# One layer of a hybrid Fourier, state-space and expert-retrieval model on one core: the context's tail reordered, the latents' first Fourier product moved behind the scores

## The reference

```
h     = RMSNorm(x) * (1 + scale1) + shift1
proj  = h @ w_in             # Fourier | z | x,B,C | dt | two gates
a_out = Re(DFT2(proj[Fourier])) @ w_fourier
y     = RMSNorm(SSD(x,B,C,dt) * silu(z)) ; b_out = y @ w_ssd_out
mix   = (sigmoid(gate_A) * a_out + sigmoid(gate_B) * b_out) @ w_out
x     = x + gate1 * RMSNorm(mix)
h     = RMSNorm(x) * (1 + scale2) + shift2
# retrieval, 8 heads: scores of two halves, top 16 of each, top 16 of their 256 sums
act   = gelu(<expert_u[idx], h>) ; out = sum(softmax(top) * act * expert_v[idx])
x     = x + gate2 * RMSNorm(out)
```

## Time and profile before

| | |
|---|---|
| median of 3 runs | 2580.18 us |
| the profiled execution | 2583.05 us, span 2581.2 us |
| granted clock of TensorE, mean | 0.956 |
| busy, share of the span | PE 89%, PEld 56%, DVE 70%, ACT 25%, POOL 46% |
| DMA | 705.28 MB, mean 273 GB/s |

### The profile page before, as it was taken

The page is one execution under the profiler, slowest core; times in us unless marked ns, Lnnn a source line. Parts: engine busy times, 40 slices in busy tenths (PEclk is TensorE's granted clock), DMA queues, the critical chain, the costliest instruction groups (busy, mean ns, idle before and its releaser), DMA issues.

```text
span 2581.2 us, 26507 instructions
## 1 busy us (share of the span) xinstructions
PE 2300.2 (89%) x8779; PEld 1451.1 (56%) x8779; DVE 1797.7 (70%) x3184; ACT 635.8 (25%) x1564; POOL 1179.9 (46%) x979
## 2 busy tenths in 40 slices
PE   6988888898899997999989999978799999999960
PEld 1545454454566443487668887856566666644420
DVE  2657676645600789778778898899676767657678
ACT  2325435231211113411322112199111111110010
POOL 0022231221000346667542235477557786876865
PEclk8999999999999998999999999999899999999985
DMA  8211101107585678999874578999999999999997
GB/s 308 74 33 58 41 24 41 49 33 296 164 284 178 213 298 324 370 369 413 320 268 160 223 280 322 351 365 412 417 379 419 378 411 409 383 400 372 414 389 288
DMA packets 235577, 705.28 MB, mean 273 GB/s; under 512 B 22910, under 2 KB 47614, under 8 KB 234052
## 3 DMA queue, kind: packets, MB, share of 16 engines
q0 software_dynamic: 117936, 429.44, 43.1%
q1 hardware_dynamic: 116948, 272.27, 28.4%
q10 hardware_dynamic: 576, 2.10, 0.2%
HBM read 690.23 MB, written 13.50 MB: 273 GB/s over the span
## 4 chain that ended last, share of the span: by engine, by line
PE 31%; DVE 22%; POOL 17%; DMA 15%; issue 11%; ACT 3%; SPq 1%; DVEq 0%; ACTq 0%; POOLq 0%
PE bank L960 13%; POOL arena L1785 7%; POOL arena L1777 7%; DMA arena<-in_peer_v,arena 6%; DMA arena<-in_peer_u,arena 6%; PE bank L809 4%; PE bank L854 2%; DVE arena L2205 2%; DVE arena L2183 2%; DVE arena L1966 2%; PE bank L1112 2%; POOL arena L1834 2%; DVE arena L2129 2%; DVE arena L2126 2%; DVE arena L2128 1%
## 5 line engine op out<-in xcount | busy, mean ns | idle before, releaser
L1777 POOL DMA_INDIRECT arena<-in_peer_u,arena x384 | 489.1, 1274 | 577.7 <-DVE arena L2183 326.5
L2205 DVE SCALAR_TENSOR_TENSOR arena<-arena 128x1024 f32<-128x1024 f32 x381 | 495.3, 1300 | 139.0 <-DMA arena<-in_peer_v,arena 134.3
L2183 DVE CUSTOM_DVE_ANT_0 arena<-arena 128x1024 f32<-128x1024 f32 x384 | 476.4, 1247 | 150.2 <-DMA arena<-in_peer_u,arena 149.6
L1785 POOL DMA_INDIRECT arena<-in_peer_v,arena x384 | 463.9, 1208 | 244.0 <-DVE arena L2205 136.8
L960 PE MATMUL bank<-arena 128*128 128x512 f32 (+1 forms) x1472 | 507.2, 507 | 15.3 <-DMA arena<-in_w_in 5.2
L1220 PE MATMUL bank<-arena 128*128 128x512 f32 x1024 | 452.3, 594 | 13.4 <-DVE arena L2381 9.3
L1182 PE MATMUL bank<-arena 128*128 128x256 f32 x2048 | 455.3, 380 | 7.1 <-ACT arena L1634 6.4
L1182 PEld LDWEIGHTS bank<-arena 128*128 128x128 f32 x2048 | 390.6, 191 | 88.4 <-issue 37.4
L960 PEld LDWEIGHTS bank<-arena 128*128 128x128 f32 x1472 | 282.4, 193 | 236.0 <-issue 201.1
L1220 PEld LDWEIGHTS bank<-arena 128*128 128x128 f32 x1024 | 195.0, 191 | 232.7 <-issue 214.4
L1634 ACT ACTIVATE arena<-bank 128x256 f32<-128x256 f32 x128 | 49.0, 383 | 589.4 <-PE bank L1182 589.4
(11 more groups left out here) (260 smaller groups left out, 2476.6 us busy)
## 6 DMA issues: line engine op xcount, KB each, us to landing
arena<-in_peer_ut SPq DMA_DIRECT2D x128, 512.0 KB, 6.5
arena<-in_peer_v SPq DMA_DIRECT2D x128, 512.0 KB, 6.6
arena<-in_w_in SPq DMA_DIRECT2D x22, 2048.0 KB, 8.1
arena<-in_w_ada_t POOLq DMA_DIRECT2D x32, 512.0 KB, 4.0
arena<-in_w_ssd_out SPq DMA_DIRECT2D x8, 2048.0 KB, 13.2
arena<-in_w_query SPq DMA_DIRECT2D x8, 2048.0 KB, 7.9
arena<-in_w_ada SPq DMA_DIRECT2D x4, 2048.0 KB, 16.3
arena<-in_w_fourier SPq DMA_DIRECT2D x4, 2048.0 KB, 7.7
```

What stands on the lines that cost most here:

```text
L1777: nc.gpsimd.indirect_dma_start(rowbuf[slot], None, a["peer_u"], bass.IndirectOffsetOnAxis(ap=entries(IDX, k), axis=0)).then_inc(row_in[slo ...
L1785: nc.gpsimd.indirect_dma_start(rowbuf[slot], None, a["peer_v"], bass.IndirectOffsetOnAxis(ap=entries(IDX, k), axis=0)).then_inc(row_in[slo ...
L2183: V.tensor_tensor_reduce(out=rowbuf[slot], in0=rowbuf[slot], in1=h2c if item < PH else h2a[:, item // PH - 1, :], scale=1.0, scalar=0.0, o ...
L2205: STT(pv, rowbuf[slot], w, pv, ALU.mult, ALU.add).then_inc(s("vc_used"), 1)
```

## The change

- The list of products: the latents' FO0 moves from behind the context's WO1 to behind its Q3. The products between change their numbers by one, and SP's loads follow.
- PE: after the Fourier stage there are no row vectors; the context's FO0 goes ahead of the transposes of Y, FO1 behind them. The four row vectors keep their order of use: kinds 0 and 1 ahead of the transposes of the merged rows, kinds 2 and 3 (four units) behind WO1, beside the norm. The latents' FO0 stands behind the scores.
- ACT: the copies move with them; kind 2 is copied between the first root and the square of x1, kind 3 behind the second root.
- DVE: the two dots of the last Fourier step come behind `put_fourier(7)`; the waits for the row vectors are split; 12 context steps stand beside the latents' FO0, three a tile, so the steps beside all later products shift by 12, and ACT's stops with them.
- Behind the scores of the latents 8 context steps are left beside the first two whole top-16 instead of 20 beside four, and the 32 apart steps stand at the third to the eighth (4, 4, 6, 6, 6, 6) instead of the fifth to the eighth (8 each).

```diff
-        + [("l", "FO0")] + [("c", f"Q{j}") for j in range(4)]
-        + [("l", n) for n in ("FO1", "GA0", ...) + STAGES]
+        + [("c", f"Q{j}") for j in range(4)]
+        + [("l", n) for n in ("FO0", "FO1", "GA0", ...) + STAGES]
-WITH = {"FO1": (2, 2, 2, 2), "GA0": (2, 2, 2, 2), ...
+WITH = {"FO0": (3, 3, 3, 3), "FO1": (2, 2, 2, 2), "GA0": (2, 2, 2, 2), ...
-CTX_BESIDE = (5, 5, 5, 5, 0, 0, 0, 0)
-APART_BESIDE = (0, 0, 0, 0, 8, 8, 8, 8)
+CTX_BESIDE = (4, 4, 0, 0, 0, 0, 0, 0)
+APART_BESIDE = (0, 0, 4, 4, 6, 6, 6, 6)
 ...
             pe.wait_ge(s("d2_free"), KT)
-            pe.wait_ge(s("coef_ready"), 3)
-            row_units(0, (2, 3), 0)
-            pe.wait_ge(s("row_free"), 4)
+            job("c", "FO0", f_lhs)
             for j in range(4):
                 pe.wait_ge(s("gt_used"), g_end("c", f"Z{j}"))
                 transpose_unit(T_YC + j, ...)
-            for j in range(2):
-                job("c", f"FO{j}", f_lhs)
+            job("c", "FO1", f_lhs)
 ...
             pe.wait_ge(s("coef_ready"), 5)
-            row_units(4, (0, 1), 0)
+            row_units(0, (0, 1), 0)
             pe.wait_ge(s("gt_used"), g_end("c", "SO3"))
-            pe.wait_ge(s("row_free"), 8)
+            pe.wait_ge(s("row_free"), 4)
 ...
             for j in range(2):
                 job("c", f"WO{j}", m_lhs)
-            job("l", "FO0", f_lhs)
+            row_units(4, (2, 3), 0)
             pe.wait_ge(s("h2_ready"), 1)
+            pe.wait_ge(s("row_free"), 8)
 ...
-            pe.wait_ge(s("tm_free"), q_end("l", "FO0"))
+            pe.wait_ge(s("tm_free"), q_end("c", "WO1"))
 ...
-            job("l", "FO1", f_lhs)
+            for j in range(2):
+                job("l", f"FO{j}", f_lhs)
 ...
@@ ACT
             root(slice(46, 47), ROOT_M[0])
+            take_rows(4, (2,), 0)
             square_x1(0)
             root(slice(51, 52), ROOT_N[0])
-            act.wait_ge(s("posm_in"), 16)
-            for i, t in enumerate(LAT4):
-                take(Q["l", "FO0"] + i, a_out(t, slice(0, 512)), ACT.Copy)
+            take_rows(6, (3,), 0)
 ...
+            act.wait_ge(s("posm_in"), 16)
+            for i, t in enumerate(LAT4):
+                between("l", "FO0", i)
+                take(Q["l", "FO0"] + i, a_out(t, slice(0, 512)), ACT.Copy)
@@ DVE
                 if f:
                     put_fourier(f - 1)
-                late_dots(DOTS_BESIDE_FOURIER[f])
+                if f < KT - 1:
+                    late_dots(DOTS_BESIDE_FOURIER[f])
             put_fourier(KT - 1)
-            late_dots(8)
+            late_dots(DOTS_BESIDE_FOURIER[KT - 1] + 8)
 ...
-            dve.wait_ge(s("row_free"), 8)
+            dve.wait_ge(s("row_free"), 4)
             add_mix(0)
+            dve.wait_ge(s("row_free"), 6)
             make_h2(0, mix_c, h2c)
             dve.wait_ge(s("sc_free"), 4)
             top(0)
             top(1)
-            for i in range(4):
-                beside("l", "FO1", i)
+            for j in range(2):
+                for i in range(4):
+                    beside("l", f"FO{j}", i)
```

More of the change, by code:

```diff
@@ L51 @@
 TAIL = ([("c", n) for n in ("Z0", "Z1", "Z2", "Z3", "FO0", "FO1", "GA0", "GA1") + STAGES]
-        + [("l", "FO0")] + [("c", f"Q{j}") for j in range(4)]
-        + [("l", n) for n in ("FO1", "GA0", "GA1", "Z0", "Z1", "Z2", "Z3") + STAGES]
+        + [("c", f"Q{j}") for j in range(4)]
+        + [("l", n) for n in ("FO0", "FO1", "GA0", "GA1", "Z0", "Z1", "Z2", "Z3") + STAGES]
         + [("l", f"Q{j}") for j in range(4)])
@@ L128 @@
 CSTEPS = PH * TOPK + LEAD
-WITH = {"FO1": (2, 2, 2, 2), "GA0": (2, 2, 2, 2), "GA1": (2, 2, 2, 2), "Z0": (2, 2, 2, 2), "Z1": (2, 2, 2, 2),
+WITH = {"FO0": (3, 3, 3, 3), "FO1": (2, 2, 2, 2), "GA0": (2, 2, 2, 2), "GA1": (2, 2, 2, 2), "Z0": (2, 2, 2, 2), "Z1": (2, 2, 2, 2),
         "Z2": (2, 2, 2, 2), "Z3": (2, 2, 2, 2), "GB0": (3, 3, 3, 3), "SO0": (2, 2, 2, 2), "SO1": (2, 2, 2, 2),
@@ L670, in _ @@
                 load_tail("c", name)
-            load_tail("l", "FO0")
             for j in range(4):
                 load_tail("c", f"Q{j}")
-            for name in ("FO1", "GA0", "GA1", "Z0", "Z1", "Z2", "Z3", "GB0", "SO0", "SO1", "GB1", "SO2", "SO3"):
+            for name in ("FO0", "FO1", "GA0", "GA1", "Z0", "Z1", "Z2", "Z3", "GB0", "SO0", "SO1", "GB1", "SO2", "SO3"):
                 load_tail("l", name)
@@ L1486, in _ @@
                 square_y(0, j)
[L1487 removed]
+            take(Q["c", "FO0"], a_out(0, slice(0, 512)), ACT.Copy)
             for j in range(4):
                 turned(T_YC + j, yTc[:, 4 * j:4 * j + 4, :], j)
[L1490 to L1491 removed]
+            take(Q["c", "FO1"], a_out(0, slice(512, 1024)), ACT.Copy)
             root(slice(30, 31), ROOT_Y["c"])
```

5 lines of the change are left out of this document (1 added, 4 removed).

## The result

| | before | after |
|---|---|---|
| median | 2579.56 us (4 runs) | 2595.82 us (4 runs, 2593.66 to 2599.43) |
| ratio | 1 | 1.0050, 95% interval 1.0026 to 1.0073 |
| profiled execution, span | 2583.05 us, 2581.2 us | 2594.78 us, 2593.0 us |

The changed kernel is slower by half a per cent: 12.9 us of 2580 by the ratio on record, 6.7 to 18.8 us by its interval; the two medians lie 16.3 us apart, inside it. The median of before counts one run more than the 2580.18 us ahead of the forecast. The forecast was 2583 us with a range of 2567 to 2597 us: the range holds the median, but the likeliest case (2576 to 2592 us) does not, and what came by the medians, "slower by over 0.5%" (a time above 2593.1 us), had 0.19.

What follows compares the result with a forecast made beforehand. The gather steps after the DVE-bound gate build set the end. PE 11.2 us late at the queries, less 6.4 at the squares, put the first gate multiply 3.8 us late: 2583 us median, range 2567 to 2597.

Steps and rivals of the forecast that it cites:

- the likeliest case: Whole kernel: DVE reaches item 2's gates late, PE stalls at Y's transposes; median 2583 us, 2576 to 2592 us, chance 0.52.
- slower by over 0.5%: Whole kernel: a time above 2593.1 us, from the slower case and the likeliest case's upper tail; chance 0.19.
- waits at the squares, PE's 6.38: Ahead of the build: ACT's 7.42 us wait for the squares goes, and with it PE's 6.38 us.
- PE's idle time: First transposes of Y: PE arrives near 984 us or a few later, idles some 20 us, resumes at 1006.9 us.
- The tail: Context's tail on PE: 4.8 us idle, 6.9 us row kinds and 1.0 us load wait saved; WO1 ends at 769.2 us.
- The norm: Behind WO1: h2's turn 9.9 us later, then 36.0 us plus 1.4 us for PE's clock; latents' FO0 at 816.5 us.
- DVE's way to item 2: From first top-16 to item 2's gates: 37.8 us of dots and adds plus 5.2 us more; reached at 999.2 us.
- the wait of step 20 stays: DVE's early steps: step 20's wait for its first rows, 4.66 us and some smaller, remains.
- Lead kept: DVE reaches Z1's gates before PE needs them; first gate multiply 1675 us, median 2570 us; chance 0.23.
- Slower: DVE never catches up; next two Y transposes stall about 7 us more each, PE 25 us late at queries, 2598 us; chance 0.17.
- The uncovered norm costs more: Context's norm costs more than the tail saves; FO1 level or 2 us late, 2585 to 2588 us; chance 0.08.

Runs made afterwards that it cites:

- the reorder alone: The changed kernel without the twelve steps beside the latents' FO0, its tail and uncovered norm kept; 2582.40 us, ratio 1.0014 to the kernel before.

## Why the prediction was right and wrong, step by step

| step | forecast | after |
|---|---|---|
| PE starts the tail's FO0 | 671.1 | 669.56 |
| WO1 ends | 769.2 | 773.03 |
| h2's turn, behind it | +9.9 | +10.2 |
| latents' FO0, first top-16 | 816.5 | 823.02, 823.00 |
| ACT's wait for item 2 ends | 999.2 | 1013.08 |
| PE takes up Y's transposes | 1006.9, idle about 20 | 1020.91, idle 18.81 |
| late at the queries | 11.2 | 23.6 |
| waits at the squares, PE's 6.38 | gone | gone |
| first gate multiply | 1689.7 | 1700.63 |
| DVE's wait ahead of it | several us | 5.31 |
| from PE's last wait of the build to the end | 757 | 753.5 |

**Right: the mechanism.** Items on third tiles, item 2 ahead of the copies of the first Y transposes, DVE two tiles further on, PE idle about 20 us, the lateness handed on to the build less the 6.4 us at the squares. Moving that one wait took 10 us back by the ratios (13 at the first gate multiply), and moving all four took 17. **Luck: PE's idle time.** Forecast about 20 us, measured 18.81, but between other ends: PE came to the transposes at 1002.1 us, not at 987, and the wait ended at 1013.08 us, not at 999.2. The forecast said that the waits at FO1 and GA1 (1 to 4 us each) would be swallowed by the big one; they were 2.48 and 8.68 us. PE's end moved by the late start and these waits, DVE's by the terms below, and the two shifts happened to be alike, 15 and 14 us. **Wrong: its size**, 3.8 us forecast at the first gate multiply and 14.7 measured. The terms:

The tail, 4 us. PE needed 103.5 us from FO0 to the end of WO1, where I had 98.1; its start 1.5 us ahead of the forecast, where the idle time was as forecast, is scatter. I let GA0's wait go; it grew to 3.54 us, and the product behind it ran 15.70 us in place of 14.20. SP's queue and two windows, of after and of before, say why (starts of the load, length to the last issue; windows as above):
```profile
676.72 23.08 SPq L656 DMA_DIRECT2D arena<-in_w_in  x3
```
```profile
677.00:691.00 14.00, 9.12 (x31) 4.39 (x29) 9.55 (x18) 6.33 (x19) 2.11 (x4) 1.00 0.96 330
691.00:707.00 16.00, 15.27 (x32) 6.28 (x30) 8.58 (x21) 2.68 (x4) 0.53 (x1) 0.89 0.78 280
```
```profile
693.00:701.00 8.00, 7.18 (x17) 2.85 (x15) 3.59 (x10) 1.36 (x3) 0.00 (x0) 1.00 0.78 262
```
GA0's weights were issued at 676.72 us, when FO0 freed their buffer, and PE had them at 690.57 us: 13.9 us, against 7.9 before (issued at 693.35 us). The earlier load runs beside the last dots' rows (512 KB each, six issued between 672 and 689 us), with the DMA share at 0.96; before, the last of these was issued at 688.54 us, ahead of the load. I had moved the load and taken its old length.

The norm, 2.4 us. After the 4.69 us idle the first query products took 17.11 us against 14.56 us at a granted clock of 0.84, 2.6 us where I had 1.4, and two query loads were waited for, not one.

DVE's way to item 2, 7.4 us. It needed 190.1 us from its first top-16, 139.7 us before (to 985.82 us), 50.4 us more; I had 43.0. The waits of that stretch, after and before, say where (engine, line, releaser: us in total, times, longest):
```profile
DVE arena L2182 <- DMA arena<-in_peer_u,arena: 14.6, 14, 2.5
DVE arena L2204 <- DMA arena<-in_peer_v,arena: 6.7, 6, 3.0
DVE arena L2201 <- DMA arena<-in_peer_v,arena: 1.3, 1, 1.3
```
```profile
DVE arena L2183 <- DMA arena<-in_peer_u,arena: 10.9, 7, 4.7
DVE arena L2202 <- DMA arena<-in_peer_v,arena: 0.7, 1, 0.7
DVE arena L2205 <- DMA arena<-in_peer_v,arena: 0.4, 1, 0.4
```
22.6 us of row waits against 12.0: the sixteen steps added wait for their rows 10.6 us, and I had counted their dots and adds only ("the wait of step 20 stays"). The 3.6 us that I gave DVE's wait for ACT's table loads did not come; that wait was 2.60 us, under the 3.80 us of before, 4.8 us less than I had, so the two mistakes partly cancel. What is left, 50.4 less the 10.6 and with the 1.2 us added back, is 41.0 us of work, where I had 39.4 (37.8 for dots and adds, 1.6 for multiplies and weights). On the table load the row stood, though I called it the time of the whole switch and it is the load's alone: each load took 1.28 us, and the activation began within 0.02 us behind it (961.70 us the load, 962.99 us the activation), and no run showed the 2.7 us that the Trainium skill, ScalarE: Activation LUTs, Rules for kernel authors, budgets for a switch.

Together 6.5 us late at the first top-16 and 7.4 more to item 2 make the 13.9 us between 999.2 and 1013.08 us. Behind it I took 1.1 us back up to the queries and the trace 2.7 (2.3 up to the start of L1179), then 6.4 at the squares as forecast, and 2.4 that I had not: behind its stall before, PE did 416 matmuls in 92.34 us, and 416 of 1024 in 221.28 us are 89.9. So 26.3 - 2.3 - 6.4 - 2.4 = 15.2 us. Behind the build the last phase was 3.6 us shorter than before, which is within its scatter.

**The rivals.** "Lead kept" fell, for the reason given against it. "Slower" came near in time (2598 us) but not in its way: the next transposes waited 3.43 us as before, so DVE did catch up. "The uncovered norm costs more" is a true cost, 8 us, which the tail's gain of 5 does not cover (the reorder alone is at 1.0014). **The bounds** were the error that mattered: for the lateness at the transposes of Y I gave 7 to 15 us, and 26.3 us were measured. Row waits could only grow with sixteen more steps in the stretch, and the three errors all had that sign; with bounds of 7 to 27 us, "slower by over 0.5%" would not have stood at 0.19.

## What to carry to other kernels

When steps are moved between engines that wait for each other in program order, count again where each wait falls: twelve steps cost 17 us here because they pushed four waits in front of work that another engine needed. A wait belongs behind the last piece of work that someone else waits for, and the cheapest test of it is to move the wait and leave the work. A load that starts earlier is a new load: look at what else is on the DMA queues at its new time before taking its old length.

## What the runs showed of the hardware

A 2 MB weight load took 7.9 us with the DMA share at 0.78 and 13.9 us at 0.96, beside the dots' row loads (512 KB each, six issued between 672 and 689 us). After 4.7 us of idle and the transposes of h2 PE ran the next 17 us at a granted clock of 0.84, where the same product had 1.00 behind a busy stretch; the mix of its two levels (1.2 and 2.4 GHz) cost 2.6 us. And PE's clock paid a little back for the missing stall: 2.4 us over 416 matmuls, at a granted clock of 1.00 (1603 to 1695 us) where before, behind its stall, it was 0.97 (1587.6 to 1680 us).
